# First unit of the second projection made inside the end of the differential heads, and two tiles' head norms moved in the recurrence

## The chip, the cores and the metric

The kernel runs on one core of a Trainium2 chip. The metric is the device time of one execution in microseconds (us). The profile is one more execution, taken by the hardware profiler. Engines: PE (TensorE; PEld is its weight load), ACT (ScalarE), DVE (VectorE), POOL (GpSimd), SP (SyncE, which issues most transfers). Matrix products are in float32; one k step of a product with 512 columns stands in the trace as two matmul records.

## The reference, cut to what matters

The reference is a first block with two layers (layer 0 and layer 1), and a second block. A layer of the first block, for 1024 tokens and 256 context tokens:

```
h = rms_norm(x) * (1 + sc) + sh
qa, ka, va, ga, qb, kb, vb, gb, qn, kn, vn, gn = split(h @ w_in)
oa = diff_attend(rope(norm(qa)), rope(norm(ka)), va)   # softmax 0 - lam * softmax 1, 4 heads
ya = rms_norm(oa, subln) * (1 - lam_init) * silu(ga)   # "mean of squares" of a
yb = gqa_attend(rope(norm(qb)), rope(norm(kb)), vb) * silu(gb)
yn = neighbourhood_attend(norm(qn), norm(kn), vn) * silu(gn)
x  = x + gate * (concat(ya, yb, yn) @ w_out)
```

In layer 0 the context tokens go through the same attention among themselves; in layer 1 they are only keys and values. The second block has a stick-breaking attention, a state-space part, a gated recurrence (hgrn2) over nine chunks of 128 tokens, and after them

```
o_hg = rmsnorm(o) * silu(g)         # per head; o_sb and o_ssd have norms of their own
h = h + concat(o_sb, o_ssd, o_hg) @ w_out
h = h + square(relu(rmsnorm(h) @ w_up)) @ w_down
```

## The kernel before, in words

Tokens are cut into tiles of 128. A stage is one `nc.Block()`; in it each engine runs its own list of instructions in order, semaphores order them between engines, and the next stage begins when all engines have ended the last. Nothing plans the order: it is written out by hand, by loops. PSUM has eight banks of 512 columns, `ps[:, 0..7, :]`. Weights come through a ring of two slots (`pr.view(i)` is chunk i, `pr.arrived` waits for its transfer, `pr.load` asks for the next once a slot is spent).

`stage_diff` (lines 1300 to 1568, once for each layer) makes the differential heads. Its units are pairs (tile t, head h): 40 in layer 0, of which the last 8 are context tiles with two key tiles each, and 32 in layer 1, all with ten key tiles. For a unit PE makes two score rows (`scores`, into banks 0 to 2 and 3 to 5), DVE takes the maxima, ACT the exponentials, DVE `combine`s the two in halves, PE transposes the result in groups of four key tiles (`transposes`, line 1413; bank 6, called TB, or bank 7, called GB, for one group near the end), ACT and DVE keep the groups (lines 1471, 1473), and for two units together PE transposes the reciprocals (line 1420) and makes the sums over the values (`weighted`, line 1428, both in bank 6). ACT copies those out (line 1492). DVE combines unit i only behind its copies of the groups of unit i - 1. Beside this PE makes the gates' columns (`project`, line 1442) in pieces, which SP sends to DRAM. The PE loop runs over s from -1 to n; for the last two s there is no gate work left. The groups of the last unit are transposed into banks 0 to 2, which only the last unit's first exponentials had to leave.

`stage_project_turned` for projection b follows at once. SP asks for the gates at its begin (lines 904, 905). ACT waits for them, takes their SiLU (line 1029), loads the table for logarithm and exponential (line 1030) and goes through the units: the square of a unit (line 1079), its root (lines 221, 222), and the squares of the differential result for the mean (`sub_square`, line 1036). DVE sums the squares, refines the root and multiplies (line 1184, semaphore `normed`). PE's list is: unit 0 (eight k steps of 512 columns, line 1003), unit 1, the first mean of squares (line 945, waits for line 1036), unit 2, the second mean, and so on. A unit's product goes to `banks[n % len(banks)]`: two banks in layer 0, four in layer 1; a unit waits until the unit before it in its bank is `normed`. With `ahead=a` the products of the first a units are left out here, since the stage before has made them: PE only raises their semaphores.

`stage_recurrence` (lines 3576 to 3921): after the projection it runs over chunks i = 1 to 8. PE makes scores, sums of decays, outputs and the state's sum (lines 3644, 3617, 3665, 3674); DVE merges scores under masks (line 3848), multiplies levels (line 3834) and updates the state (line 3863); POOL multiplies the key levels (line 3800). The head norms of output tiles 0 and 1 are done in its course: `early[i] = t` lets ACT square tile t at the end of iteration i; in iteration i + 1 ACT takes the root, DVE makes `heads_mean` (lines 2401 to 2406) between the two merges and `heads_scale` (lines 225 to 228, 2419 to 2422) at the end, and POOL `heads_gain` (line 2427). The other six tiles are done in `stage_out`.

`layer` calls the projections; the call for b gives no `ahead`, so it is 0.

Of the kernel before, what the change touches and what calls it, by code (L numbers as in the profile page):

```python
# [20 lines left out]
P = 128  # L21
D = 1024
KC = D // P
# [1276 lines left out]
def stage_diff(pr, tiles, qk, V, P1, P2, PT, OA, lam, w, ident, gates):  # L1300

    nc, S, ps = pr.nc, pr.S, pr.ps
    i0 = pr.next_use
    flat = ps[:].rearrange("p b n -> p (b n)")
    st, rb, ro = w["st"], w["rb"], w["ro"]
    hT, raw, spill = gates["hT"], gates["raw"], gates["spill"]
    units = [(t, h) for t in tiles for h in range(AH)]
    n = len(units)
    nk = [NT if t < XT else CT for t, h in units]
    ng = [-(-k // 4) for k in nk]  # L1310
    TB, GB = 6, 7
# [5 lines left out]
    quanta = []  # L1317
# [27 lines left out]

    def bank_of(i, g):

        return g if i == n - 1 else GB if i == n - 2 and g == 1 else TB

    def last_in_TB(j):  # L1350
        return max((i for i in range(j) if uses[i][0] == "pair" or bank_of(*uses[i][1:]) == TB), default=None)
# [11 lines left out]
    def full_units(i):  # L1363
        return sum(t < XT for t, h in units[:i + 1])

    def halves_combined(i):
        return sum(1 + (k > 4) for k in nk[:i + 1])

    with nc.Block() as block:
# [8 lines left out]
        @block.tensor  # L1378
        def _(pe):
            def scores(i):  # L1380
                t, h = units[i]
                if i >= 1:
                    pe.wait_ge(*S["exps_0"](i))
                    pe.wait_ge(*S["exps_1"](i))

                def score(half, m, at, width, key):
                    r = slice(64 * m + 32 * half, 64 * m + 32 * half + 32)
                    return pe.matmul(flat[:, 3 * m * BANK + at:3 * m * BANK + at + width], qk[r, h, t * P:(t + 1) * P],  # L1388
                                     qk[r, AH + h, key:key + width], start=True, stop=True)

                if t >= XT:
                    for m in range(2):
                        score(0, m, 0, CTX, SEQ).then_inc(*S[f"scored_{m}"].inc())
                    return
                for m in range(2):
                    score(1, m, 2 * BANK + P, P, SEQ + P).then_inc(*S["shared_begun"].inc())
                for m in range(2):
                    score(0, m, 0, BANK, 0).then_inc(*S[f"scored_{m}"].inc())
                for m in range(2):
                    score(1, m, BANK, BANK, BANK).then_inc(*S[f"scored_{m}"].inc())  # L1400
                pe.wait_ge(*S["shared_begun"](2 * full_units(i)))
                for m in range(2):
                    score(0, m, 2 * BANK, P, SEQ).then_inc(*S[f"scored_{m}"].inc())

            def transposes(i, g):
                j = place["unit", i, g]
                pe.wait_ge(*S["combined"](halves_combined(i - 1) + 1 if g == 0 else halves_combined(i)))
                if bank_of(i, g) == GB:
                    pe.wait_ge(*S["gate_kept"](len(pieces)))
                elif bank_of(i, g) == TB and j:  # L1410
                    turned_away(pe, last_in_TB(j))
                for b in range(4 * g, min(4 * g + 4, nk[i])):
                    mm = pe.transpose(ps[:, bank_of(i, g), (b % 4) * P:(b % 4 + 1) * P], P1[:, i % 3, b * P:(b + 1) * P], ident)  # L1413
                mm.then_inc(*S["pT_ready"].inc())

            def weighted(pair):
                j = place["pair", pair, 0]
                pe.wait_ge(*S["rb_ready"](pair + 1))
                turned_away(pe, last_in_TB(j))
                pe.transpose(R_AT, rb[:, pair % 2, :], ident).then_inc(*S["r_ready"].inc())  # L1420
                for e in range(2):
                    for g in range(ng[2 * pair + e]):
                        turned_away(pe, place["unit", 2 * pair + e, g])
                t, h = units[2 * pair]
                kt = list(range(NT)) if t < XT else list(range(XT, NT))
                for b, key in enumerate(kt):
                    for e in range(2):
                        mm = pe.matmul(O_AT[64 * e:64 * e + 64, :], V[:, key, (h + e) * HD:(h + e + 1) * HD],
                                       PT[(2 * pair + e) % 4][:, b, :], start=(b == 0), stop=(b == len(kt) - 1))
                        if b == len(kt) - 1:  # L1430
                            mm.then_inc(*S["o_ready"].inc())

            def project(part):
                for i, k in part:
                    b, lo, hi = pieces[i]
                    c = b // 4
                    if k == 0:
                        if i in chunk_begins:
                            pr.arrived(pe, i0 + c)
                        if i:  # L1440
                            pe.wait_ge(*S["gate_kept"](i))
                    mm = pe.matmul(ps[:, GB, 0:hi - lo], pr.view(i0 + c)[:, k, b % 4 * P:(b % 4 + 1) * P], hT[:, k, lo:hi],  # L1442
                                   start=(k == 0), stop=(k == KC - 1))
                    if k == KC - 1:
                        mm.then_inc(*S["gate_done"].inc())
                        if i in chunk_ends:
                            pe.wait_ge(*S["gate_done"](i + 1))
                            pe.sem_inc(pr.spent, 1)

            for s in range(-1, n + 1):  # L1450
                part = quanta[s + 1] if s + 1 < n else []
                third = len(part) // 4
                cuts = [part[0:third], part[third:3 * third], part[3 * third:]]
                if s >= 3 and s % 2 == 1:
                    weighted(s // 2 - 1)
                if s + 1 < n:
                    scores(s + 1)
                for g in range(3):
                    if s >= 1 and g < ng[s - 1]:
                        transposes(s - 1, g)  # L1460
                    project(cuts[g])
            weighted(n // 2 - 1)

        def keep_group(eng, i, g):
# [2111 lines left out]
def stage_recurrence(pr, hT, qk, Kt, LF, c, rot, sg, Vh, OH, b_, hn):  # L3576


    nc, S, ps = pr.nc, pr.S, pr.ps
    EX, Qt, Kl, EE, kend, Sm, st, dec = (b_[k] for k in ("EX", "Qt", "Kl", "EE", "kend", "Sm", "state", "decay"))  # L3580
    i0 = pr.next_use
    n = L2T
# [1 line left out]
    LOG_TINY = math.log(1e-30)  # L3584
    LAG = 1
    place = lambda m, fb: 2 * m + fb + 1
    early = {n - 5: 0, n - 4: 1}
    turned = lambda t: ps[:, {n - 2: 2, n - 1: 1}[t] if t >= n - 2 else 4, :]
    sums_bank = lambda i: 6 if i < 2 else 0
    with nc.Block() as block:  # L3590
# [373 lines left out]
def layer(pr, l, io, T, const, x_src, ctx_src, dst, nx, loads, lead=None):  # L3964

    nc, S = pr.nc, pr.S
    hT, YT, small, mod = (T[k] for k in ("hT", "YT", "small", "mod"))
    last = l == LAYERS - 1
# [29 lines left out]
    def small_work(w, name):  # L3998
# [4 lines left out]
    s, qk, V = project("a", 8, AH * HD, lambda qk, V: {  # L4003
        "heads": [{"chunk": 0, "dst": qk, "b0": 0, "dim": DIFF_D, "n_heads": 16, "span": only_k_a,
                   "blocks": lambda t: tuple(h // 2 for h in only_k_a(t)),
                   "gain": [(gains[:, 0, 0:DIFF_D], 0, 8), (gains[:, 1, 0:DIFF_D], 8, 16)], "places": twice_place,
                   "rope": rope_a, "tiles": every}],
        "copy": {"chunk": 1, "lo": 0, "hi": 256, "dst": V}}, 2 * BANK, True, banks=lambda sb: (0, 1, 6, 7),
        ahead=lambda sb: 2 if l else BEGUN, later=lambda sb: (1, 2, 2, 2) if last else ())
    with s, ExitStack() as w:  # L4010
        sb = lambda nm, shape: w.enter_context(nc.sbuf_tensor(f"{nm}_a_{l}", shape, F32))
        later = YT[:, 2:KC, :].rearrange("p k n -> p (k n)")
# [24 lines left out]
    width = pieces[-1][1]  # L4037

    def norm_of_a(sb):
# [6 lines left out]
    s, qk, V = project("b", 4, BKV * HD, lambda qk, V: {  # L4046
        "heads": [{"chunk": 0, "dst": qk, "b0": 0, "dim": HD, "n_heads": 8, "span": only_k_b,
                   "blocks": lambda t: tuple(h // 2 for h in only_k_b(t)),
                   "gain": [(gains[:, 2, :], 0, BH), (gains[:, 3, :], BH, 8)], "places": plain_place(HD),
                   "rope": rope_b, "tiles": every}],  # L4050
        "copy": {"chunk": 1, "lo": 0, "hi": 128, "dst": V}}, BANK, True,
        banks=lambda sb: (0, 1, 6, 7) if last else (0, 1), later=lambda sb: (2, 4, 4, 4) if last else (), raw=lambda sb: (YT[:, 2:KC, 0:width], io["spill"][:, 2:KC, 0:width]), sub=norm_of_a,
        silu=lambda sb: [YT[:, k, 0:pieces[-1][1]] for k in range(2, 5)], **({} if last else {"ada": modulate}))
    raw = T["raw"].rearrange("p a n -> p (a n)")
    blocks_of_4 = lambda ap: ap.rearrange("p (k n) -> p k n", k=4)
# [11 lines left out]
    with s, ExitStack() as w:  # L4067
        sb = lambda nm, shape: w.enter_context(nc.sbuf_tensor(f"{nm}_b_{l}", shape, F32))
# [25 lines left out]
    def load_bias(sp):  # L4094
# [10 lines left out]
        banks=lambda sb: (0, 1, 3, 5), gate=gating, spare=lambda sb: (RPB_W // P, load_bias),  # L4105
        silu=lambda sb: [YT[:, k, 0:pieces[-1][1]] for k in range(5, KC)])
    with s, ExitStack() as w:
        sb = lambda nm, shape: w.enter_context(nc.sbuf_tensor(f"{nm}_c_{l}", shape, F32))
# [17 lines left out]
    with outer, ExitStack() as w:  # L4126
        sb = lambda nm, shape: w.enter_context(nc.sbuf_tensor(f"{nm}_{l}", shape, F32))
# [207 lines left out]
```

## Time and profile before

| | |
|---|---|
| median of 3 runs | 3634.17 us (3634.16 to 3634.7) |
| the profiled execution | 3634.86 us |
| its span | 3633.1 us |
| instructions in the span | 53890 |
| PE, DVE, ACT, POOL busy | 97%, 63%, 35%, 29% of the span |

The span runs from the first to the last instruction of the profiled execution; the rest of its time lies around it. The rows that follow further down have the start in us from the span's begin, the length in us (of a merged row: from the first start to the last end), the engine, line and operation, what it wrote and read, the count, and in brackets how long the engine stood idle before it and what ended the wait.

### The profile page before, as it was taken

To read this page: it belongs to the slowest core of one execution; us is meant where nothing else is said; L and a number is where in the kernel's file an instruction comes from. 1 tells how busy PE (TensorE), PEld (TensorE's weight loads), DVE (VectorE), ACT (ScalarE), POOL (GpSimd) and SP (SyncE) were. 2 spreads that over 40 slices of the span, in tenths; PEclk is the share of its full clock that TensorE was granted. 3 is DMA by queue.
4 is the path that set the end of the run, shared out by engine and by line. 5 is a ranking of instruction groups with operands and counts; after the bars stand their busy time and mean duration, and the time that the engine had idled before them with its cause. 6 is when DMAs were issued, how large, how long until landed. Compare 5 with 4: busy or idle time off the path is not lost. (4 is left out here: it accounts for less than half of the span.)

```text
span 3633.1 us, 53890 instructions
## 1 busy us (share of the span) xinstructions
PE 3522.3 (97%) x20756; PEld 2534.5 (70%) x20756; DVE 2282.5 (63%) x4223; ACT 1268.5 (35%) x2394; POOL 1045.3 (29%) x981
## 2 busy tenths in 40 slices
PE   7999998999999999989999999999998999999999
PEld 4656546789754655567898568555655588888888
DVE  4277454765675377557656662575658776894488
ACT  3255434532632255446425321575332211001100
POOL 2400063666541500256665430001234200000000
PEclk9999999999999999999999999999999999999999
DMA  5101143001112101110011221000000376552254
GB/s 200 50 18 42 48 156 102 2 1 42 54 62 93 47 18 42 64 36 1 2 41 55 81 82 36 24 24 24 24 24 26 114 281 252 186 188 91 93 185 162
DMA packets 142267, 279.01 MB, mean 77 GB/s; under 512 B 5728, under 2 KB 50784, under 8 KB 139584
## 3 DMA queue, kind: packets, MB, share of 16 engines
q1 hardware_dynamic: 114848, 221.89, 17.6%
q10 hardware_dynamic: 25872, 47.71, 3.7%
q0 software_dynamic: 1296, 5.97, 0.4%
q8 instruction: 168, 2.75, 0.3%
q14 instruction: 83, 0.68, 0.1%
HBM read 231.52 MB, written 44.04 MB: 76 GB/s over the span
## 5 line engine op out<-in xcount | busy, mean ns | idle before, releaser
L1003 PE MATMUL ps<-ring,hT 128*128 128x512 f32 (+3 forms) x1296 | 375.8, 446 | 9.5 <-DVE nrm_b L1184 4.4
L1003 PEld LDWEIGHTS ps<-ring,hT 128*128 128x128 f32 x1296 | 217.9, 191 | 145.9 <-issue 122.9
L1544 DVE TENSOR_REDUCE stat_a<-ps 128x1 f32<-128x1280 f32 (+1 forms) x144 | 190.7, 1366 | 153.8 <-PE ps L1388 153.8
L1442 PE MATMUL ps<-hT,ring 128*128 128x512 f32 (+1 forms) x640 | 280.2, 551 | 0.0
L1753 POOL TENSOR_TENSOR P_b<-P_b,stat_b 128x1280 f32<-128x1280 f32 (+1 forms) x108 | 227.7, 2130 | 173.9 <-DVE stat_b L1769 135.7
L2842 ACT ACTIVATE hid<-hid 128x1024 f32<-128x1024 f32 x32 | 33.8, 1057 | 482.5 <-DVE hid L2889 425.7
L1484 ACT ACTIVATE YT<-ps,stat_a 128x1280 f32<-128x1280 f32 (+1 forms) x144 | 176.5, 1231 | 25.4 <-DVE stat_a L1544 25.4
L2669 PE MATMUL ps<-Y 128*128 128x256 f32 x768 | 171.1, 379 | 0.9 <-DVE Y L2654 0.5
L1528 POOL COPY rb_a<-stat_a 128x64 f32<-128x64 f32 x72 | 14.6, 236 | 538.8 <-DVE YT L1557 538.8
L2669 PEld LDWEIGHTS ps<-Y 128*128 128x128 f32 x768 | 145.8, 190 | 21.3 <-issue 1.5
L1413 PEld LDWEIGHTS ps<-const,YT 128*128 128x128 f32 x656 | 71.6, 142 | 97.4 <-issue 86.5
L1672 PE MATMUL ps<-const,P_b 128*128 128x128 f32 x984 | 130.3, 279 | 5.9 <-POOL P_b L1753 4.5
L1726 ACT ACTIVATE P_b<-ps,stat_b 128x1280 f32<-128x1280 f32 (+1 forms) x108 | 132.8, 1236 | 3.9 <-DVE stat_b L1784 2.8
L1442 PEld LDWEIGHTS ps<-hT,ring 128*128 128x128 f32 x640 | 106.3, 191 | 39.3 <-issue 36.3
L1716 ACT ACTIVATE PT_b<-ps 128x512 f32<-128x512 f32 x146 | 82.0, 596 | 146.0 <-PE ps L1672 146.0
L3125 PE MATMUL ps<-hT,ring 128*128 128x348 f32 (+1 forms) x384 | 129.4, 466 | 0.0
L1672 PEld LDWEIGHTS ps<-const,P_b 128*128 128x128 f32 x984 | 105.9, 141 | 32.1 <-issue 24.4
L1635 PE MATMUL ps<-qk_b 64*128 64x512 f32 (+1 forms) x590 | 119.6, 532 | 4.5 <-ACT P_b L1726 2.6
L1683 PE MATMUL ps<-PT_b,v_b 128*64 128x128 f32 x1968 | 120.2, 276 | 3.5 <-DVE YT L1765 1.8
L3424 POOL TENSOR_SCALAR aU_ssd<-const,sc_ssd 128x128 f32<-128x128 f32 x64 | 44.5, 711 | 266.6 <-DVE sc_ssd L3440 231.4
L1683 PEld LDWEIGHTS ps<-PT_b,v_b 128*64 128x64 f32 x1968 | 107.0, 137 | 13.1 <-issue 9.4
L2669 PE MATMUL ps<-hT,ring 128*128 128x256 f32 x512 | 115.7, 379 | 0.0
(614 smaller groups left out, 8130.1 us busy)
## 6 DMA issues: line engine op xcount, KB each, us to landing
ring<-in_w_up SPq DMA_DIRECT2D x16, 2048.0 KB, 9.2
ring<-down_sums SPq DMA_DIRECT2D x16, 2048.0 KB, 8.2
ring<-in_w_in SPq DMA_DIRECT2D x14, 2048.0 KB, 8.1
ring<-in_w_down SPq DMA_DIRECT2D x12, 2048.0 KB, 8.2
adaw_b<-in_w_ada SPq DMA_DIRECT2D x16, 1024.0 KB, 5.2
ring<-in_w_out SPq DMA_DIRECT2D x6, 2048.0 KB, 8.1
Wd<-in_w_down ACTq DMA_DIRECT2D x11, 1024.0 KB, 7.3
down_sums<-Wd ACTq DMA_DIRECT2D x11, 1024.0 KB, 7.3
```

The lines of the kernel that those rows point to most:

```text
L1003: mm = pe.matmul(ps[:, bank(n), 0:hi - lo], hT[:, k, t * P:(t + 1) * P], w[:, k, lo:hi], start=(k == 0), stop=(k == KC - 1))
L1442: mm = pe.matmul(ps[:, GB, 0:hi - lo], pr.view(i0 + c)[:, k, b % 4 * P:(b % 4 + 1) * P], hT[:, k, lo:hi], start=(k == 0), stop=(k == KC - 1))
L1484: act.activation(dst, scored_at(i, m), ACT.Exp, bias=st[:, i % 4, m:m + 1], accum_out=st[:, i % 4, 2 + m:3 + m])\
L1544: dve.tensor_reduce(st[:, i % 4, m:m + 1], scored_at(i, m), AX, ALU.max, negate=True)\
L1635: return pe.matmul(flat[:, at:at + width], qk[r, u["qb"], u["qt"] * P:(u["qt"] + 1) * P], qk[r, u["kb"], key:key + width], start=True, sto ...
L1672: mm = pe.transpose(ps[:, bank, (i - lo) * P:(i - lo + 1) * P], weights(p, e)[:, b * P:(b + 1) * P], ident)
L1683: mm = pe.matmul(O_AT[64 * e:64 * e + 64, :], V[:, key, u["v0"] + e * HD:u["v0"] + (e + 1) * HD], turned(p, e * nk[p] + b, e * nk[p] + b + ...
L1716: eng.activation(dst, src, ACT.Copy).then_inc(*S["pT_kept_act"].inc())
L1726: act.activation(weights(p, e), scored_at(p, e), ACT.Exp, bias=st[:, p % 8, e:e + 1], accum_out=st[:, p % 8, 2 + e:3 + e]).then_inc(*S["ex ...
L1753: pool.tensor_tensor(weights(p, e), weights(p, e), st[:, p % 8, 4 + e:5 + e].to_broadcast([P, nk[p] * P]), ALU.mult)\
L2669: mm = pe.matmul(pr.ps[:, bank, at], a[:, k, :], b[:, k, :], start=(k == 0), stop=(k == 3))
L3125: mm = pe.matmul(ps[:, dense_bank(u), 0:hi - lo], w[:, k, (b % 4) * P:(b % 4 + 1) * P], hT[:, k, lo:hi], start=(k == 0), stop=(k == KC - 1))
```

## The change

The first part concerns `stage_diff` and the call for projection b. Unit 0 of projection b (tile 0) is made in bank 0 at the end of `stage_diff`: two k steps behind the last but one pair's sums, two behind the first group of unit n - 2, one behind its other groups, one behind the first group of unit n - 1, and two behind its other groups. It waits for the weights and for the last unit's first exponentials. The last unit's groups go to banks 3 to 5. Projection b is called with `ahead=1`.

The second part is one line: tile 0 is squared at the end of iteration 2 and normed in iteration 3, where it was 4 and 5; tile 1 at the end of iteration 4 and in iteration 5, where it was 5 and 6.

```diff
     def bank_of(i, g):
-        return g if i == n - 1 else GB if i == n - 2 and g == 1 else TB
+        return 3 + g if i == n - 1 else GB if i == n - 2 and g == 1 else TB
...
-            for s in range(-1, n + 1):
-                part = quanta[s + 1] if s + 1 < n else []
+            def next_unit(ks):
+                w = pr.view(i0 + 2)
+                if ks[0] == 0:
+                    pr.arrived(pe, i0 + 2)
+                    pe.wait_ge(*S["exps_0"](n))
+                for k in ks:
+                    pe.matmul(ps[:, 0, :], hT[:, k, 0:P], w[:, k, :], start=(k == 0), stop=(k == KC - 1))
+
+            for s in range(-1, n - 1):
+                part = quanta[s + 1]
...
-                if s + 1 < n:
-                    scores(s + 1)
+                scores(s + 1)
                 for g in range(3):
                     if s >= 1 and g < ng[s - 1]:
                         transposes(s - 1, g)
                     project(cuts[g])
+            weighted(n // 2 - 2)
+            next_unit([0, 1])
+            for g in range(ng[n - 2]):
+                transposes(n - 2, g)
+                if g == 0:
+                    next_unit([2, 3])
+            next_unit([4])
+            for g in range(ng[n - 1]):
+                transposes(n - 1, g)
+                if g == 0:
+                    next_unit([5])
+            next_unit([6, 7])
             weighted(n // 2 - 1)
...
-    early = {n - 5: 0, n - 4: 1}
+    early = {n - 7: 0, n - 5: 1}
...
-        banks=lambda sb: (0, 1, 6, 7) if last else (0, 1), later=...
+        banks=lambda sb: (0, 1, 6, 7) if last else (0, 1), ahead=lambda sb: 1, later=...
```

## Rows read from the trace of the kernel before

**Rows 1.** The page's busy table: busy us, share of the span, instructions.
```profile
PE 3522.3 (97%) x20756; PEld 2534.5 (70%) x20756; DVE 2282.5 (63%) x4223; ACT 1268.5 (35%) x2394; POOL 1045.3 (29%) x981
```

**Rows 2.** Timeline of PE, layer 0, stage_diff's end and projection b's start.
```profile
443.54 0.66 PE L1428 MATMUL ps<-PT_a,v_a 128*64 128x128 f32 x8
444.84 0.63 PE L1413 MATMUL ps<-const,YT 128*128 128x128 f32 x4 [0.65 <-ACT ro_a L1492]
445.82 0.30 PE L1420 MATMUL ps<-const,rb_a 128*128 128x128 f32 x1 [0.35 <-ACT PT_a L1471]
...
446.48 0.27 PE L1428 MATMUL ps<-YT,v_a 128*64 128x128 f32 x1
448.11 15.67 PE L1003 MATMUL ps<-ring,hT 128*128 128x512 f32 x32 [1.36 <-PEq L1369]
463.62 1.02 PE L945 MATMUL ps<-sub_sq_b,const 128*128 128x512 f32 x2
464.47 0.59 PE L1003 MATMUL ps<-ring,hT 128*128 128x512 f32 x1
```

**Rows 3.** Timeline of PE, layer 1, the same place.
```profile
1497.29 2.40 PE L1428 MATMUL ps<-PT_a,v_a 128*64 128x128 f32 x40
...
1503.86 2.47 PE L1413 MATMUL ps<-const,YT 128*128 128x128 f32 x10 [1.73 <-DVE YT L1557]
...
1510.43 0.27 PE L1428 MATMUL ps<-YT,v_a 128*64 128x128 f32 x1
1512.08 13.97 PE L1003 MATMUL ps<-ring,hT 128*128 128x512 f32 x32 [1.38 <-PEq L1369]
1525.88 1.02 PE L945 MATMUL ps<-sub_sq_b,const 128*128 128x512 f32 x2
```

**Rows 4.** Timeline of ACT, layer 0, projection b's start.
```profile
454.34 2.43 ACT L1029 ACTIVATE gates_b<-gates_b 128x1280 f32<-128x1280 f32 x2 [4.99 <-DMA gates_b<-gates]
...
458.08 0.60 ACT L1079 ACTIVATE sq_b<-ps 128x512 f32<-128x512 f32 x1
...
460.52 0.61 ACT L1036 ACTIVATE sub_sq_b<-YT 128x512 f32<-128x512 f32 x1
```

**Rows 5.** Timeline of ACT, layer 1, projection b's start.
```profile
1522.52 0.61 ACT L1036 ACTIVATE sub_sq_b<-YT 128x512 f32<-128x512 f32 x1
```

**Rows 6.** Timeline of DVE, layer 0, projection b's start.
```profile
462.48 0.69 DVE L1184 TENSOR_TENSOR nrm_b<-ps,st_b 128x512 f32<-128x512 f32 x1
```

**Rows 7.** Timeline of DVE, layer 1, stage_diff's end.
```profile
1501.42 1.17 DVE L1473 COPY PT_a<-ps 128x512 f32<-128x512 f32 x2 [3.12 <-PE ps L1413]
...
1503.05 1.68 DVE L1557 SCALAR_TENSOR_TENSOR YT<-YT,stat_a 128x512 f32<-128x512 f32 x2
```

**Rows 8.** Windows: us, PE busy (records), granted clock, DMA share, GB/s.
```profile
448.20:451.60 3.40, 3.40 (x5) 0.50 0.77 227
1499.60:1502.90 3.30, 1.56 (x12) 1.00 0.51 152
1503.00:1509.70 6.70, 5.45 (x37) 0.50 0.00 1
```

**Rows 9.** Timeline of PE in the recurrence, chunks 4 to 6.
```profile
2721.55 2.07 PE L3644 MATMUL ps<-hT 64*128 64x128 f32 x28
...
2739.21 2.07 PE L3644 MATMUL ps<-hT 64*128 64x128 f32 x28 [1.06 <-DVE Sm_hgc L3848]
...
2746.87 2.07 PE L3644 MATMUL ps<-hT 64*128 64x128 f32 x28 [1.56 <-DVE Sm_hgc L3848]
...
2751.14 1.00 PE L3665 MATMUL ps<-V,Sm_hgc 128*128 128x64 f32 x8
2755.27 3.34 PE L3644 MATMUL ps<-hT 64*128 64x128 f32 x28 [3.13 <-DVE Sm_hgc L3848]
```

**Rows 10.** Timeline of DVE in the recurrence, chunk 6.
```profile
2750.56 0.42 DVE L2401 TENSOR_REDUCE hst<-hT 128x4 f32<-128x256 f32 x1
...
2752.39 2.74 DVE L3848 COPY_PREDICATED Sm_hgc<-const,ps 128x512 f32<-128x512 int32 x4 [0.21 <-DVE hst L2406]
```

More of the change, by code:

```diff
@@ L4051, in layer @@
         "copy": {"chunk": 1, "lo": 0, "hi": 128, "dst": V}}, BANK, True,
-        banks=lambda sb: (0, 1, 6, 7) if last else (0, 1), later=lambda sb: (2, 4, 4, 4) if last else (), raw=lambda sb: (YT[:, 2:KC, 0:width], io["spill"][:, 2:KC, 0:width]), sub=norm_of_a,
+        banks=lambda sb: (0, 1, 6, 7) if last else (0, 1), ahead=lambda sb: 1, later=lambda sb: (2, 4, 4, 4) if last else (), raw=lambda sb: (YT[:, 2:KC, 0:width], io["spill"][:, 2:KC, 0:width]), sub=norm_of_a,
         silu=lambda sb: [YT[:, k, 0:pieces[-1][1]] for k in range(2, 5)], **({} if last else {"ada": modulate}))
```

## The prediction

> **What bounds the kernel now.** I read the page's busy table first: the reader is to see TensorE (PE) at 97% of the span [rows 1]. So time changes only where PE stands still, or where its own work grows or shrinks. The change touches three places, the end of the differential stage with the start of the next projection in layer 0, the same in layer 1, and the recurrence of the second block. For each I read PE's timeline, then the timelines of the engines that PE waits for.
>
> Layer 0 [rows 2]: the last but one pair's sums end at 443.54 + 0.66 = 444.20 us, PE stands 0.65 us and 0.35 us around four transposes, the last pair ends at 446.48 + 0.27 = 446.75, and the projection's first matmul is at 448.11 (call such a start S). 32 records, two units, follow; then the first mean of squares at 463.62 and the third unit at 464.47.
>
> Layer 1 [rows 3]: sums until 1497.29 + 2.40 = 1499.69, transposes in small lots until the last lot of ten at 1503.86, the last pair's sums until 1510.70, S at 1512.08. Some 6 us of this is PE idle or slow.
>
> The start of the projection is the decisive view. There ScalarE does not wait for PE [rows 4, 5]: it waits for the gates' transfer, takes their SiLU until 456.77, loads a table, squares unit 0 at 458.08, and its squares for the first mean end at 460.52 + 0.61 = 461.13, which is S + 13.0. VectorE's norm of unit 0 ends at 462.48 + 0.69 = 463.17, S + 15.1 [rows 6]. In layer 1 those squares end at 1523.13, S + 11.05.
>
> **The change, part by part.** It removes eight k steps of unit 0 from behind S and puts them ahead. 32 records at full clock take 13.97 us, pipeline end included, so a unit is about 6.86 us, 0.86 us for each step [rows 3].
>
> *Tail, layer 0.* The stage's PE idle is 0.65 + 0.35 us [rows 2] and the inserted work is 6.86 us. With 0.35 us of pipeline drain that is filled as well, the last sums end 6.86 - 1.0 - 0.35 = 5.5 us later, and S with them, as all engines meet there. The bounds are 4.3 (twice the idle) and 6.86 (none filled).
>
> *Start, layer 0.* PE is in order: unit 1, the first mean of squares, unit 2. Projection b has two banks here, so unit 2 waits for unit 0's norm. Both other engines' chains begin at S with the transfer, so they move by 5.5 us. Unit 2 goes from 464.47 to 463.17 + 0.13 + 5.5 = 468.8: the 6.86 us that left give back 1.2 us, and this layer stands at +4.3 us. Behind the waiting mean and unit 2 all later matmuls of the stage are queued on PE, and they follow it without larger gaps, so nothing takes this back. The bounds are +5.5 - 6.86 - 1.7 = -3.1 (no chain holds, and the slow clock of 448.2 to 451.6 goes too) and +5.5 (nothing given back).
>
> *Tail, layer 1.* Here the order matters. PE does steps 0 and 1 from about 1499.45 to 1501.2, unit 30's first transposes to 1501.6, steps 2 and 3 to 1503.3, its other six to 1504.0. VectorE copies two of these three groups before it combines unit 31; those copies ended at 1501.42 + 1.17 = 1502.59 [rows 7] and end at about 1504.95 now. The first half of the combined unit, 1.3 us behind the copies, comes at 1506.2 in place of 1503.9; the last pair follows with steps 5, 6 and 7 in between and ends at about 1512.65, against 1510.70. So S moves by 1.95 us. Bounds: -1.5 (all hidden, and the half clock of the last sums gone) and +5.5 (as in layer 0).
>
> *Start, layer 1.* The first mean was at 1525.88. Its squares now end at 1523.13 + 1.95, and with 0.2 us for the weight load it starts at 1525.3, 0.6 us earlier. Four banks mean that unit 2 needs no norm. So the start takes back 2.55 of the 6.86 us that left. Tail and start net: -0.6 us, bounds 1.95 - 6.86 = -4.9 (no chain holds) and +1.95 (nothing given back).
>
> *Clock at both starts.* PE is now idle from S + 6.9 to S + 13.0 in layer 0 and from S + 6.9 to S + 11.1 in layer 1. In the trace the granted clock was 0.50 (1.2 GHz) for 3.4 us behind the thin tail of layer 0, which costs 1.7 us, and for 6.7 us in layer 1, where PE had been busy 1.56 of 3.3 us before: 3.35 us [rows 8]. The two new waits are at least as empty. I take 1.2 us in layer 0, where part of the slow time would lie beside the wait for the norm, and 1.7 in layer 1; bounds 0 to 1.7 and 0 to 3.35.
>
> The Trainium skill, "TensorE: Matmul & The Clock Gate", Part 1, says that the throttled state is the default and that activity releases it; the trace's two falls behind thin stretches agree. By that rule both new waits are paid for as above; if they cost no clock, the whole sum is 2.9 us smaller.
>
> *Recurrence.* The work of a tile's head norms is the same; it moves from chunks 5 and 6 to 3 and 5. A plain iteration's PE has no wait there (28 matmuls, 2.07 us) [rows 9]. The first tile made PE wait 1.06 us for VectorE in its own iteration and 1.56 us at the next; the second added a wait of 3.13 us and 1.27 us of half clock: 7.0 us for both. When tile 1 no longer stands in the iteration behind, the merge that held PE starts at 2750.56, where that tile's reductions began, not at 2752.39 [rows 10]. PE's third wait, which began at 2751.14 + 1.0, ends 1.83 us earlier and is 1.3 us. One tile alone then costs 1.06 + 1.56 + 1.3 = 3.9 us, two 7.8: +0.8 us, of which I take 0.7 (the slow clock cost a little beyond the 28). Bounds: -4.9 (1.06 each) and +4.5 (1.06 + 1.56 + 3.13 each). The other moves of that edit, ScalarE's squares and GpSimd's gain, go with the tile and are in the same waits; no transfer moves.
>
> *At nothing:* the bank of the last transposes (3 to 5 for 0 to 2) was read last by the exponentials that the combining waits for anyway; the weights of the new unit were asked for in the middle of the stage; the wait for the last unit's first exponentials is over before PE reaches it, as PE first has the last but one pair's sums to do, 2.40 us in layer 1 [rows 3]. If that cover failed, each would hold PE for some 0.65 us, as ScalarE's copy does in [rows 2].
>
> Sum: layer 0 +4.3 + 1.2, layer 1 +1.95 - 2.55 + 1.7, which is +1.1, recurrence +0.7: +7.3 us. The profiled execution took 3634.86 us, its span 3633.1 and 1.8 around it; the median is 0.7 lower, so 3634.2 + 7.3 = 3641.5.
>
> **The rivals.**
> 1. *Faster: PE's time goes out in full.* If the start chain of ScalarE did not hold PE, both units vanish behind S: -13.7, tails +7.45, layer 0's slow clock -1.7, recurrence +0.7: -7.3, that is 3626.9. It would decide from the point where the squares for the first mean come by S + 6.9. Against it: they come at S + 13.0 and S + 11.05, with ScalarE waiting for a transfer that is issued only at S [rows 4, 5]. For it: PE is what bounds the whole. Chance 0.08.
> 2. *The spread tiles are absorbed.* VectorE catches up in the free iteration between, and each tile costs only its first wait: the recurrence gives -4.9 in place of +0.7, in all +1.7: 3635.9. For it: the worst wait came with the second tile in a row. Against it: the 1.56 us behind the first tile comes before the second has done anything on VectorE. Chance 0.17.
> 3. *The clock falls everywhere.* Both starts pay their upper bound, and PE's short wait in layer 1's tail (about 1.4 us before 1506.2) lets the last sums run slow again, 1.4 us: +0.5 + 1.65 + 1.4, in all about +10.9: 3645. Chance 0.17.
>
> **How the numbers follow.** Forecast 0.58, rivals 0.08, 0.17, 0.17. A measurement of this kernel tells a change from none from about 0.2% on, 7.3 us, which is where the forecast itself lies: its own range, 3638 to 3645, falls nearly evenly to both sides, 0.28 to "same" and 0.30 to slower. With rival 2 same is 0.45, with rival 3 slower 0.47, rival 1 leaves 0.08 for faster. The range 3631 to 3648 leaves out rival 1 and tails of the unknown terms.
>
> **What would show it.** In the profile after: S about 5.5 us and 2 us later; behind unit 1 a PE wait on the mean's squares of 6 and 4 us, in layer 0 a second one on the norm; granted clock 0.50 behind them and no longer ahead of S; in the recurrence two pairs of iterations with waits near 1 and 1.5 us and none of 3. It is wrong if PE goes from unit 1 to the mean without a wait, or if S hardly moves in layer 0.

## The result and the profile after

The changed kernel takes 3645.35 us (median of 8 runs, 3643.96 to 3647.39), the kernel before 3635.05 us in the same comparison (8 runs, 3631.89 to 3636.62): ratio 1.0029, 95% interval 1.002 to 1.0038. It is slower by 10.3 us; 3641.5 was forecast, with a range of 3631 to 3648. The profiled execution took 3643.96 us with a span of 3642.2, that is 9.1 us more than the span before; all sums below go by this pair.

The busy table after (columns as in [rows 1]):

```profile
PE 3528.0 (97%) x20756; PEld 2536.4 (70%) x20756; DVE 2284.7 (63%) x4223; ACT 1268.5 (35%) x2394; POOL 1045.2 (29%) x981
```

The same number of instructions on every engine, and PE is busy 5.7 us longer than in [rows 1], with stretches at half clock that are shown below. The rest of the 9.1 us is PE standing still. Where both lie is read from the start of each stage on PE, before and after (us):

```
stage starts at                  before     after   later by   this stretch
differential, layer 0            165.27    165.58      0.31        +0.31
projection b, layer 0 (S)        448.11    454.29      6.18        +5.87
next stage, layer 0              574.60    579.77      5.17        -1.01
differential, layer 1           1263.13   1268.24      5.11        -0.06
projection b, layer 1 (S)       1512.08   1519.68      7.60        +2.49
next stage, layer 1             1604.27   1612.63      8.36        +0.76
recurrence                      2607.14   2615.52      8.38        +0.02
stage behind the recurrence     2781.90   2791.26      9.36        +0.98
```

Layer 0 costs 5.87 - 1.01 = 4.86 us, layer 1 2.49 + 0.76 = 3.25 us, the recurrence 0.98 us; the other stretches moved by 0.3 us at most.

PE's timeline after, layer 0, which answers to [rows 2] (L1456 is the unit made ahead; L1003 is projection b):

```profile
444.48 1.98 PE L1456 MATMUL ps<-ring,hT 128*128 128x512 f32 x4
446.30 0.38 PE L1413 MATMUL ps<-const,YT 128*128 128x128 f32 x2
446.52 2.74 PE L1456 MATMUL ps<-ring,hT 128*128 128x512 f32 x6
...
452.48 0.27 PE L1428 MATMUL ps<-YT,v_a 128*64 128x128 f32 x1
454.29 7.10 PE L1003 MATMUL ps<-ring,hT 128*128 128x512 f32 x16 [1.53 <-PEq L1369]
466.63 2.08 PE L945 MATMUL ps<-sub_sq_b,const 128*128 128x512 f32 x2 [5.24 <-ACT sub_sq_b L1036]
468.66 8.05 PE L1003 MATMUL ps<-ring,hT 128*128 128x512 f32 x16
```

The tail is gap-free now, so the weights of the new unit and the exponentials, which the prediction put at nothing, did cost nothing; the 32 records of the start have become 16, and where the other 16 stood PE waits 5.24 us for ScalarE's squares. The third unit starts at 468.66; in [rows 2] it started at 464.47. The work went out, and a wait came in its place. PE's row has no second wait ahead of the third unit, because the slow mean lasts until 468.71, but the unit's weight load (PEld) has one, for VectorE's norm:

```profile
468.66 0.50 PEld L1003 LDWEIGHTS ps<-ring,hT 128*128 128x128 f32 x2 [1.53 <-DVE nrm_b L1184]
```

The engines it waits for, ScalarE and VectorE in the same stretch, after [rows 4, 6]:

```profile
459.81 2.43 ACT L1029 ACTIVATE gates_b<-gates_b 128x1280 f32<-128x1280 f32 x2 [4.43 <-DMA gates_b<-gates]
...
463.56 0.60 ACT L1079 ACTIVATE sq_b<-ps 128x512 f32<-128x512 f32 x1
...
465.96 0.61 ACT L1036 ACTIVATE sub_sq_b<-YT 128x512 f32<-128x512 f32 x1
...
467.92 0.69 DVE L1184 TENSOR_TENSOR nrm_b<-ps,st_b 128x512 f32<-128x512 f32 x1
```

ScalarE does what it did before, in the same order and nearly as long after S: gates, their SiLU, the first squares. These squares end at 466.57, S + 12.3 (S + 13.0 before).

Layer 1, PE after, which answers to [rows 3]:

```profile
1505.01 1.98 PE L1456 MATMUL ps<-ring,hT 128*128 128x512 f32 x4
...
1511.81 0.66 PE L1413 MATMUL ps<-const,YT 128*128 128x128 f32 x4 [1.15 <-DVE YT L1576]
...
1519.68 7.11 PE L1003 MATMUL ps<-ring,hT 128*128 128x512 f32 x16 [1.53 <-PEq L1369]
1530.79 1.12 PE L945 MATMUL ps<-sub_sq_b,const 128*128 128x512 f32 x2 [4.00 <-ACT sub_sq_b L1036]
1531.75 8.73 PE L1003 MATMUL ps<-ring,hT 128*128 128x512 f32 x16
```

The same unit before:

```profile
1526.74 7.03 PE L1003 MATMUL ps<-ring,hT 128*128 128x512 f32 x16
```

The same picture: a wait of 4.00 us for the squares, and behind it a unit that takes 8.73 us in place of 7.03. The windows of PE after (columns as in [rows 8]) say why:

```profile
454.00:461.00 7.00, 6.71 (x16) 1.00 0.87 329
461.00:467.50 6.50, 1.26 (x2) 0.71 1.06 454
467.50:469.50 2.00, 2.00 (x3) 0.50 0.69 245
1511.00:1516.00 5.00, 4.19 (x21) 1.00 0.00 0
1516.00:1519.00 3.00, 2.15 (x40) 1.00 0.00 0
1527.00:1533.00 6.00, 2.21 (x4) 0.92 0.78 311
1533.00:1536.00 3.00, 3.00 (x5) 0.58 0.00 0
1586.50:1590.00 3.50, 3.50 (x20) 0.53 0.74 254
1596.80:1600.20 3.40, 3.40 (x18) 0.52 0.00 0
```

The granted clock falls to 0.50 (1.2 GHz) behind the new wait of layer 0, and a window behind that of layer 1 is at 0.58 in the mean. It no longer falls ahead of S: the last sums of layer 1 ran at half clock in [rows 8], and the windows 1511 to 1516 and 1516 to 1519 of after are at 1.00. The last two rows are a place that the prediction did not look at, the end of projection b in layer 1. PE there, first before, then after:

```profile
1578.81 0.66 PE L956 MATMUL ps<-const,rot_b 128*128 128x128 f32 x4 [2.37 <-POOL rot_b L1285]
1579.31 3.74 PE L1003 MATMUL ps<-ring,hT 128*128 128x128 f32 x32
1584.56 2.05 PE L1003 MATMUL ps<-ring,hT 128*128 128x128 f32 x16 [1.52 <-DVE nrm_b L1184]
1586.45 0.60 PE L956 MATMUL ps<-const,rot_b 128*128 128x128 f32 x4
1589.91 5.62 PE L1003 MATMUL ps<-ring,hT 128*128 128x128 f32 x48 [2.86 <-DVE nrm_b L1184]
1595.37 0.60 PE L956 MATMUL ps<-const,rot_b 128*128 128x128 f32 x4
```

```profile
1585.53 0.66 PE L956 MATMUL ps<-const,rot_b 128*128 128x128 f32 x4 [2.38 <-POOL rot_b L1285]
1586.02 7.31 PE L1003 MATMUL ps<-ring,hT 128*128 128x128 f32 x48
1593.16 0.60 PE L956 MATMUL ps<-const,rot_b 128*128 128x128 f32 x4
1596.64 7.25 PE L1003 MATMUL ps<-ring,hT 128*128 128x128 f32 x48 [2.87 <-DVE nrm_b L1184]
1603.72 0.60 PE L956 MATMUL ps<-const,rot_b 128*128 128x128 f32 x4
```

The waits for GpSimd's and VectorE's last work are the same (2.4 and 2.9 us), but after the change the clock fell behind both. The first fall cost nothing: it stands in place of a wait of 1.52 us, and PE is 6.72 us later ahead of it (1585.53 against 1578.81) and 6.71 us later behind it (1593.16 against 1586.45). The second cost 1.6 us: from 6.73 us later (1596.64) to 8.35 us later (1603.72).

The recurrence after, PE, which answers to [rows 9]:

```profile
2724.83 2.07 PE L3663 MATMUL ps<-hT 64*128 64x128 f32 x28 [1.06 <-DVE Sm_hgc L3867]
...
2732.48 2.85 PE L3663 MATMUL ps<-hT 64*128 64x128 f32 x28 [1.56 <-DVE Sm_hgc L3867]
...
2739.29 2.07 PE L3663 MATMUL ps<-hT 64*128 64x128 f32 x28
...
2751.64 2.07 PE L3663 MATMUL ps<-hT 64*128 64x128 f32 x28 [1.06 <-DVE Sm_hgc L3867]
...
2759.30 2.41 PE L3663 MATMUL ps<-hT 64*128 64x128 f32 x28 [1.56 <-DVE Sm_hgc L3867]
...
2766.13 2.07 PE L3663 MATMUL ps<-hT 64*128 64x128 f32 x28
```

Two pairs of waits of 1.06 and 1.56 us, and none of 3.13. Behind each second wait PE runs a stretch at half clock (2.85 and 2.41 us for the 28 records in place of 2.07); the third iteration then has no wait left. VectorE's last merge of masks before that third iteration, in the first tile:

```profile
2736.17 2.73 DVE L3867 COPY_PREDICATED Sm_hgc<-const,ps 128x512 f32<-128x512 int32 x4
```

### The profile page after: what moved, and what is told of

Its sections match the earlier page's. It is cut to its first block and busy times, and to the rows that moved or that the text cites. A ratio compares the mean times of both kernels' runs of the same rounds, so it can differ in the third digit from the quotient of the medians.

```text
span 3642.2 us, 53894 instructions
## 1 busy us (share of the span) xinstructions
PE 3528.0 (97%) x20756; PEld 2536.4 (70%) x20756; DVE 2284.7 (63%) x4223; ACT 1268.5 (35%) x2394; POOL 1045.2 (29%) x981
## 3 DMA queue, kind: packets, MB, share of 16 engines
q1 hardware_dynamic: 114848, 221.89, 17.5%
## 5 line engine op out<-in xcount | busy, mean ns | idle before, releaser
L1003 PE MATMUL ps<-ring,hT 128*128 128x512 f32 (+3 forms) x1264 | 366.2, 447 | 8.4 <-PEq L1369 3.1
L1003 PEld LDWEIGHTS ps<-ring,hT 128*128 128x128 f32 x1264 | 215.3, 195 | 138.6 <-issue 115.7
```

Of the source, the lines that this page charges most:

```text
L1003: mm = pe.matmul(ps[:, bank(n), 0:hi - lo], hT[:, k, t * P:(t + 1) * P], w[:, k, lo:hi], start=(k == 0), stop=(k == KC - 1))
```

## The experiments

Each was timed in 5 rounds, the first four on one chip beside 29 runs of the kernel before (median 3634.46), the other four on another beside 33 (3634.95).

**e1: the recurrence alone.** The kernel before with one line:

```
-    early = {n - 5: 0, n - 4: 1}
+    early = {n - 7: 0, n - 5: 1}
```

> The kernel before with the one line of the recurrence (tiles 0 and 1 normed in chunks 3 and 5). Theory (VectorE is late by about 4 us for each tile, wherever the tile stands): +1 us, between 0 and +1.7, with PE waits of 1.06 and 1.56 us behind each tile and none of 3. Rival A (spreading the tiles lets VectorE catch up): -4 to -5 us. Rival B (this line is the larger part of the loss): +5 us or more.

3635.82 us (11 runs), ratio 1.0003 (0.9994 to 1.0012); from the recurrence's start to the next stage it took 175.79 us, against 174.76 in before and 175.74 in the changed kernel. PE waits 1.06 and 1.54 us for the first tile, 1.05 and 1.55 for the second, and none of 3, as was expected. In the trace the line costs about 1 us, which the interval of the medians does not tell from nothing; it gains nothing. The tiles are not absorbed by a free iteration between them.

**e2: the unit alone.** The changed kernel with that line as it was before.

> The changed kernel with the recurrence's line undone: only the unit of projection b in the tail of the differential stage. Theory (ScalarE's chain at the projection's start sets when PE gets on, and PE has nothing to do meanwhile): +8.1 us, 7 to 9.5. Rival A of the first kernel: +13 (as the line would be a gain). Rival B: +3 to +5.

3644.38 us (7 runs), ratio 1.0028 (1.0017 to 1.0039): +9.9 us, a little over the 7 to 9.5 expected. So nearly all of the loss is the unit's. Its ledger in the two layers is like that of the changed kernel: S 5.80 us later in layer 0 and 2.47 in layer 1 (counted from the start of the differential stage), layer 0 as a whole +4.04, layer 1 +3.79, and the two waits at the end of layer 1's projection (2.38 and 2.86 us) both followed by slow matmuls again. The profiled execution was the slowest of the seven: its recurrence took 3.19 us longer than before's with the same line, and the stretch ahead of the recurrence 1.70.

**e3: the unit made twice.** e2, and the start makes the unit again, so that nothing leaves it:

```
-        ahead=lambda sb: 1, ...
+        ahead=lambda sb: 0, ...
```

> As the one before, but the projection makes its unit 0 again: the tail's work is added and nothing is taken away behind it, the result of the tail is overwritten. Theory: the removal of unit 0 gave back only 2 to 2.5 us at each start, and what follows ran at half clock; with unit 0 made again PE is busy until the first mean, so the time is +5 to +7 against before, that is no slower than the kernel that makes unit 0 once, rather 1 to 3 us faster. Rival (the 6.86 us of each unit were taken off the time, the tail's cost hid it): 13.7 us slower than the kernel that makes it once, +22.

3642.24 us (11 runs), ratio 1.002 (1.0011 to 1.0029), +7.8 us where 5 to 7 were expected: 2.1 us less than with the unit made once, though PE has two units more to do. The intervals of e2 and e3 overlap, but the rival's 13.7 us more lie far outside both. PE at the start of layer 0:

```profile
454.60 13.97 PE L1003 MATMUL ps<-ring,hT 128*128 128x512 f32 x32 [1.39 <-PEq L1369]
468.41 1.02 PE L945 MATMUL ps<-sub_sq_b,const 128*128 128x512 f32 x2
```

No wait, and full clock. The first mean starts at S + 13.8 with 32 records ahead of it and started at S + 12.3 with 16 in the changed kernel, where it and the unit behind it then ran slow (2.08 and 8.05 us, here 1.02 and 7.06). So the 13.7 us that the change took out of the starts were worth nothing: PE's time there is set by ScalarE, and behind the idle time PE ran slow. What slows the kernel is the tail: in e3's trace S comes 5.68 us later in layer 0 and 2.08 in layer 1.

**e4: the gates later.** If ScalarE's first squares came by S + 6.9, the gain should appear. e2, with the gates' wait and SiLU behind the second unit's squares on ScalarE, and GpSimd's products with the gates behind two of its rotations:

```
-            if sub:
+            def gates_of_a():
                 act.wait_ge(*S["sub_gates_in"](16))
...
+                act.preload_act_table_set(LN_EXP)
...
                         sub_square(m)
+                    if sub and m == 1:
+                        gates_of_a()
...
             for r, (m, j, t) in enumerate(turned):
+                for i, (c, lo, hi) in enumerate(spans if r == 2 else ()):
...
```

> The unit in the tail (recurrence as before), and at projection b's start ScalarE takes the gates' SiLU behind unit 1 and GpSimd multiplies the gates behind unit 1's rope, so that nothing stands between S and unit 0's square. Theory: S is late by 5.7 and 2.5 us as in the changed kernel, but now 6.86 us each come back, and the slow clock at layer 0's start (1.6 us) is gone: -7 us against before, -4 to -9. Rival (the loss lies in the tail and in the clock, not in ScalarE's order): no better than the kernel with the unit alone, +6 to +9.

3633.44 us (11 runs), ratio 0.9996 (0.9987 to 1.0005): 1.0 us less than before, and 7 were expected. The step itself did as reckoned, but the gain was given back further on. ScalarE's first squares, PE, both in layer 0, and the transfers issued from 452 to 475 us (KB each, median us from issue to landing):

```profile
456.80 0.61 ACT L1038 ACTIVATE sub_sq_b<-YT 128x512 f32<-128x512 f32 x1
```

```profile
453.78 7.11 PE L1003 MATMUL ps<-ring,hT 128*128 128x512 f32 x16 [1.53 <-PEq L1373]
460.72 1.02 PE L945 MATMUL ps<-sub_sq_b,const 128*128 128x512 f32 x2
461.58 7.03 PE L1003 MATMUL ps<-ring,hT 128*128 128x512 f32 x16
...
472.03 1.07 PE L263 MATMUL ps<-adaw_b,cs 128*32 128x256 f32 x16 [2.13 <-DMA adaw_b<-in_w_ada]
```

```profile
YT<-gates SPq DMA_DIRECT2D x1, 3840.0 KB, 14.9
adaw_b<-in_w_ada SPq DMA_DIRECT2D x3, 1024.0 KB, 17.5
```

The squares end at S + 3.6, the wait for them is gone, and the third unit starts 2.9 us before its time of [rows 2]. But the modulation's weights are on SyncE's queue behind 3.8 MB of other gates, and PE, which now comes earlier, waits 2.13 us for them. Layer 0 kept 0.99 us; a stretch at half clock at 593 us took 1.6 more; layer 1, which has no modulation here, gained 2.89; the recurrence took 2.17 us longer in this execution, with its old line.

**e5: the control.** The same order of gates, without the unit: the kernel before with the lines of e4 alone.

> A control: the kernel before, with nothing in the tail, but with ScalarE's gates' SiLU behind unit 1 and GpSimd's multiplication of the gates behind unit 1's rope. Theory (before the change PE never waited for ScalarE at the projection's start, so the new order buys nothing by itself): 0, between -1.5 and +1.5 us. Rival (the new order is the gain, with or without the unit): as the kernel with unit and order, and 2 us or more below the kernel before.

3633.87 us (11 runs), ratio 0.9997 (0.9988 to 1.0006). The order alone moves nothing that can be told (-1.1 us), and nor does e4 (-1.0). So e5 does not show a gain that needs both; it shows that with the new order the unit costs nothing (e4 against e5), where it cost 9.9 us with the old one (e2). In e5's trace layer 0 is 2.14 us shorter than in before. Of this, 1.70 is a slow stretch behind S that this execution does not have: its 32 records take 13.97 us, and 15.67 in before.

**e6, e8 and e7: the new wait removed.** e8 is e4 with the first two of the modulation's loads ahead of the 3.8 MB on SyncE's queue; e6 is e8 with the recurrence's new line; e7 is e8 with the unit made ahead in layer 1 only.

```
-                sp.dma_start(*raw).then_inc(*S["gates_in"].inc(16))
+                if not jobs:
+                    sp.dma_start(*raw).then_inc(*S["gates_in"].inc(16))
             for a in range(jobs):
+                if a == 2 and raw:
+                    sp.dma_start(*raw).then_inc(*S["gates_in"].inc(16))
```

> Unit in the tail, new order on ScalarE and GpSimd, recurrence in chunks 3 and 5, and in layer 0 the first two loads of the modulation's weights asked for before the other gates (3.8 MB) in place of behind them. Theory: the wait of 2.13 us on those weights behind unit 2 goes, so 1 to 2 us less than the kernel with the new order alone, the recurrence's line within 1 us either way: -2 to -5 us against before. Rival (the weights' loads keep a rate that holds PE further on): no better than that kernel, -1.

> As the kernel with unit, order and loads, but with the recurrence's tiles in chunks 5 and 6 as before. Theory (the line is worth +1 us, less than the stage's own spread of 3 us between executions): within 1.5 us of it. Rival (spread tiles are a gain that the slow clock hid): 2 us or more slower than it.

> The unit in the tail of layer 1 alone, new order and loads in both layers, recurrence as before. Theory: layer 0's tail costs 5.7 us and its unit gives back 6.86 and a slow clock of 1.6, so leaving it out loses some 2.8 us against the kernel with the unit in both layers and the same order and loads, and stands at -3 to 0 against before. Rival (layer 0's tail with its 1 us of PE idle is no place for the unit): equal or faster.

e6: 3630.9 us, 0.9987 (0.9978 to 0.9996), 3.0 us further below its before than e4, where 1 to 2 were expected. e8: 3630.26 us, 0.9983 (0.9975 to 0.9992). e7: 3631.19 us, 0.9987 (0.9978 to 0.9996); 11 runs each. PE in e8, layer 0:

```profile
452.95 7.11 PE L1006 MATMUL ps<-ring,hT 128*128 128x512 f32 x16 [1.54 <-PEq L1376]
459.90 1.02 PE L948 MATMUL ps<-sub_sq_b,const 128*128 128x512 f32 x2
460.76 7.03 PE L1006 MATMUL ps<-ring,hT 128*128 128x512 f32 x16
...
469.01 1.07 PE L263 MATMUL ps<-adaw_b,cs 128*32 128x256 f32 x16
```

Neither wait is left. In e6's trace layer 0 gains 3.31 us and layer 1 4.33, 7.6 in all; its recurrence takes 2.26 us longer than before's, and 4.05 us are left in the medians. e8 and e6 differ by 0.6 us, as was expected for the recurrence's line. e7 is only 0.9 us behind e8, where 2.8 were expected: the unit of layer 0 by itself is worth about 1 us, which these intervals do not tell from nothing. e8 has the lowest median, 4.7 us under the kernel before; e6 and e7 cannot be told from it. The changed kernel is 10.3 us over the kernel before.

No version has the new order and the loads without the unit, so the medians do not say what those two give alone. The traces do in part. Layer 1 has no modulation, so the loads change nothing there: with the order alone (e5) it is 0.40 us longer than in before, with the order and the unit (e6, e8) 4.33 shorter (2.89 and 2.81 in e4 and e7, where the clock fell behind the wait of 2.9 us at its end). In layer 0, order and loads without the unit (e7) give 0.62 us, with it 3.31 (e6) and 2.91 (e8). With the gates' order and the loads changed, making the unit ahead pays, in layer 1 clearly; without them it costs.

## Why the prediction was right, and where its sizes were off

The sign, the main mechanism (the start's wait for ScalarE) and the range held; the clock at the second start was mis-sized, and the recurrence's third wait was not there. Step by step, in the profiled pair:

- *Tail, layer 0:* +5.5 forecast, +5.87 measured; of the difference 0.17 is the longer gap ahead of S (1.53 against 1.36 us). The idle was filled and the rest of the unit paid, as reckoned. The lower bound, "twice the idle", is 4.5 by its own terms and not 4.3; the sum does not use it.
- *Start, layer 0:* it was to give back 1.2 us and gave back 5.87 - (468.66 - 464.47 - 0.31) = 2.0. The wait on the norm set unit 2 as forecast (the norm ends at 468.61, unit 2 starts at 468.66, 0.05 us behind it where 0.13 was taken), but the chain from S to the norm's end took 14.3 us in place of 15.1; 0.56 us of that is the shorter wait for the gates' transfer (4.43 against 4.99).
- *Clock, layer 0:* 1.2 forecast. Unit 2 took 8.05 in place of 7.03 us: 1.02. The slow mean (2.08 us) lay beside the wait for the norm, and cost nothing, as was assumed.
- *Tail, layer 1:* 1.95 forecast, 2.49 measured. The copies came 0.6 us later than reckoned (the end of 1509.62 + 1.02, less the 5.11 us brought along, is 1505.53 and not 1504.95), and everything behind them with them. The last sums ran at full clock.
- *Start, layer 1:* 2.55 given back forecast; the mean at 1530.79 against 1525.88 is 0.20 us early against its old place, so 2.69.
- *Clock, layer 1: the term that was mis-sized.* 1.7 forecast; 1.8 came at the start (0.1 in the mean, 1.7 in unit 2), and 1.6 more at the end of the same projection. The sum counted the clock only at the new waits. Its upper bound, 3.35, was also misread: in the 6.7 us of [rows 8] PE was busy 5.45, so half clock cost PE's own work at most 2.7. The waits of 2.4 and 2.9 us that were there before are followed by slow matmuls after the change. Together with the tail that is the layer's +3.25 in place of +1.1.
- *Recurrence:* +0.7 forecast, +0.98 measured. The third wait of 1.3 us did not come: a stretch at half clock behind the second one stood in its place and cost 1.7 us (in the first tile 0.78 + 0.26 + 0.62 on three groups). The merge that PE would have waited for ended at 2736.17 + 2.73 = 2738.90; without the slow stretch PE would have come to it at 2739.29 - 1.66 = 2737.63, so by estimate a wait of about 1.3 us was there, hidden by the slow stretch. The forecast of two pairs of waits and none of 3 us was right; that the size came out so near is in part luck, as a term that the sum did not have stood in for one that it had.

The sum: 4.86 + 3.25 + 0.98 = 9.1 against 7.3. The clock (1.5 us over) and the tails (0.9 over) were partly made up for by the starts, which gave back 0.9 more than forecast. The other 1.2 us of the measured 10.3 are the spread of single executions around their medians (the profiled one of after is the fastest of its 8).

Rival 1 fell, and e4, e6 and e8 show that its condition was named rightly: with the squares early enough PE's time does go out. In e6's trace the start of layer 0 gives back 9.16 us and that of layer 1 6.85, that is both units (6.86 each), layer 0's slow clock (1.7) and 0.6 more; less the tails of 5.85 and 2.52 this leaves 7.6 us, where rival 1 reckoned 8.0 for the two layers. It took the removal of a second wait, and in the medians e6 and e8 keep 4.1 and 4.7. Rival 2 fell by e1: +1.4 us, where it named 4.9 us of gain in the recurrence. Rival 3 named nearly the measured time (3645), but not by its mechanism: it had the last sums of layer 1's tail run slow, and they ran at full clock; what came in their place lay at the end of the projection.

**What stays open.** Why the clock falls behind the two old waits at the end of layer 1's projection in some executions and not in others. In the trace of before neither wait has a fall behind it; of the six other versions that make the unit ahead or make it twice, e2 and e7 have a fall behind both, e3, e4 and e6 behind one, e8 behind none; the profile is one execution of each. The stretch at half clock behind S in layer 0 is as uneven: before, e1 and e7 have it, e5, with the same tail, does not. So is the recurrence: with its old line it took 174.74 to 177.95 us in before, e2 to e5, e7 and e8. The three long ones, e2 to e4, have a slow stretch behind the wait of 1.56 us, and then waits of 1.5, 1.1 and 1.3 us in place of one of 3.1; all three ran on one chip, and e5, e7 and e8 on the other, so whether the chip or the execution makes the difference is not shown. That alone is 3 us, a third of the loss and two thirds of what e8 gains.

## What to carry to other kernels

Work moved ahead of a stage on the busiest engine pays only as far as the next thing on that engine isn't set by another engine's chain that begins where the stage begins: follow that chain from the stage's start, and count the wait that takes the work's place. Making the work twice is a cheap test of that, since where it costs nothing, PE's time was not the bound. And once the chain is shortened, look on the DMA queue for what the earlier engine will ask for next: here layer 0 kept 0.99 us of gain with two loads behind the large one (e4) and 3.31 with them ahead of it (e6), in one profiled execution of each.

## What the runs showed of the hardware

The granted clock is not a fixed price of a wait: the same wait of 2.9 us was followed by 5.62 us for 48 records in before and by 7.25 us in after. The Trainium skill, "TensorE: Matmul & The Clock Gate", Part 1, has the throttled state as the default that activity releases; the falls behind both new waits agree with that (5.24 us idle, then 0.50; 4.00 us idle, then a unit of 8.73 us in place of 7.03). The old waits show that the same idle time can end either way. Twice a slow stretch cost nothing because it stood where a wait would have been (the 1.52 us at 1584.56 of before, and the slow mean of layer 0).

A transfer's time depends on what stands ahead of it on its queue: the modulation's 1 MB landed 5.2 us after its issue as the median of the whole kernel. At the start of projection b in layer 0 it took 17.5 us with the loads behind 3.8 MB (e4) and 8.7 with two of them ahead of it (e8), each the median of three.
